# Block 2: log gates one panel earlier, first softmax ahead of a weight remainder, decays inside the attention, squares added before they are summed

## The reference, cut to what matters

```python
# block 1 (RWKV + dilated attention + FFN), then block 2, two layers of
h = h + 0.5 * rmsnorm(swiglu(rmsnorm(h, g_pre_ffn1), w_ffn1_gu, w_ffn1_down), g_post_ffn1)
h = h + rmsnorm(token_mixer(rmsnorm(h, g_pre_mix), ...), g_post_mix)
h = h + 0.5 * rmsnorm(swiglu(rmsnorm(h, g_pre_ffn2), w_ffn2_gu, w_ffn2_down), g_post_ffn2)
# token_mixer
fq, fk, fv, ff, gq, gk, gv, ga, gr, g_merge_a, g_merge_b = split(h @ w_in)
log_f = log_sigmoid(ff + b_f)                         # forget gates, 8 heads
o_fox = fox_attention(fq, fk, fv, cumsum(log_f))      # softmax attention, 3 blocks of queries
log_a = log_sigmoid(ga @ w_alpha_up + b_alpha) / 16   # decays of the gated linear attention
o_gla = gla_chunked(gq, gk, gv, log_a)                # uses exp of cumsum(log_a), per chunk
y = (sigmoid(g_merge_a) * (o_fox @ w_fox_o) + sigmoid(g_merge_b) * (o_gla @ w_gla_o)) @ w_out
```

## Time and profile before

| | before |
|---|---|
| median of 3 runs | 2022.82 us (2022.75, 2022.82, 2027.86) |
| the profiled execution | 2027.96 us, its span 2026.1 us |
| PE busy | 1910.9 us, 94% |
| DVE busy | 1402.3 us, 69% |
| ACT busy | 908.5 us, 45% |
| POOL busy | 102.4 us, 5% |

### The profile page before, as it was taken

How to read it: one execution, slowest core, us unless ns; L and a number is a source line. 1 busy time by engine, 2 the same in 40 slices (tenths; PEclk the granted TensorE clock), 3 DMA queues, 4 the chain that set the end, 5 groups by cost and what they waited for, 6 DMA issues and landing times.

```text
span 2026.1 us, 36336 instructions
## 1 busy us (share of the span) xinstructions
PE 1910.9 (94%) x14822; PEld 1860.5 (92%) x14822; DVE 1402.3 (69%) x2171; ACT 908.5 (45%) x1345; POOL 102.4 (5%) x164
## 2 busy tenths in 40 slices
PE   7897899998799999999899999999999989999997
PEld 7896788988799999999899999999999989999997
DVE  6997576677766567656767777756765676777764
ACT  3443444443555454444546444434443454544442
POOL 0201021200000000002100000000000200000000
PEclk7998888998899999999999999999999999999999
DMA  9684020003355535553323535543554333454552
GB/s 359 254 307 152 31 75 1 1 1 128 118 183 190 193 136 176 181 193 126 115 103 110 178 136 180 188 170 128 184 182 174 132 101 109 146 187 146 186 194 98
DMA packets 41435, 301.47 MB, mean 149 GB/s; under 512 B 4512, under 2 KB 6704, under 8 KB 7264
## 3 DMA queue, kind: packets, MB, share of 16 engines
q1 hardware_dynamic: 40720, 296.90, 41.6%
q0 software_dynamic: 592, 2.87, 0.4%
HBM read 298.70 MB, written 1.05 MB: 148 GB/s over the span
## 4 chain that ended last, share of the span: by engine, by line
PE 79%; DVE 12%; DVEq 4%; ACT 2%; issue 1%; DMA 1%; POOL 0%; SPq 0%; ACTq 0%; POOLq 0%
PE acc L718 20%; PE acc L720 19%; PE acc L719 19%; DVE w_lo L700 3%; ACT w_hi L693 1%; PE acc L744 1%; PE acc L745 1%; PE acc L748 1%; PE mb L733 1%; PE mb L720 1%; PE mb L718 1%; PE mb L719 1%; PE mb L2048 1%; PE acc L2048 1%; DVEq L858 1%
## 5 line engine op out<-in xcount | busy, mean ns | idle before, releaser
L718 PE MATMUL acc<-h_hi,w_hi 128*128 128x272 f32 (+1 forms) x2752 | 795.0, 289 | 22.0 <-DVE w_lo L700 12.1
L720 PE MATMUL acc<-h_hi,w_lo 128*128 128x272 f32 (+1 forms) x2752 | 788.1, 286 | 0.0
L719 PE MATMUL acc<-h_lo,w_hi 128*128 128x272 f32 (+1 forms) x2752 | 786.6, 286 | 0.0
L700 DVE TENSOR_TENSOR w_lo<-land,w_hi 128x2048 fp32r<-128x2048 f32 (+1 forms) x243 | 586.2, 2412 | 148.9 <-ACT w_hi L693 148.1
L693 ACT ACTIVATE w_hi<-land 128x2048 fp32r<-128x2048 f32 (+1 forms) x243 | 488.6, 2011 | 429.6 <-PE acc L720 376.9
L718 PEld LDWEIGHTS acc<-h_hi,w_hi 128*128 128x128 f32 x2752 | 522.7, 190 | 27.3 <-DVE w_lo L700 14.5
L719 PEld LDWEIGHTS acc<-h_lo,w_hi 128*128 128x128 f32 x2752 | 522.2, 190 | 0.4 <-issue 0.2
L720 PEld LDWEIGHTS acc<-h_hi,w_lo 128*128 128x128 f32 x2752 | 522.6, 190 | 0.0
L718 PE MATMUL acc<-a_hi,w_hi 128*128 128x272 f32 (+1 forms) x880 | 251.7, 286 | 0.7 <-DVE w_lo L700 0.5
L719 PE MATMUL acc<-a_lo,w_hi 128*128 128x272 f32 (+1 forms) x880 | 250.3, 284 | 0.0
L720 PE MATMUL acc<-a_hi,w_lo 128*128 128x272 f32 (+1 forms) x880 | 250.3, 284 | 0.0
(11 more groups left out here) (560 smaller groups left out, 2785.6 us busy)
## 6 DMA issues: line engine op xcount, KB each, us to landing
land<-in_w_gu SPq DMA_DIRECT2D x110, 1024.0 KB, 4.8
land<-in_w_in SPq DMA_DIRECT2D x67, 1024.0 KB, 4.8
land<-in_w_down SPq DMA_DIRECT2D x40, 1408.0 KB, 6.0
ada_first<-in_w_ada SPq DMA_DIRECT2D x24, 1024.0 KB, 8.4
land<-in_w_ab SPq DMA_DIRECT2D x12, 1024.0 KB, 4.9
land<-in_w_out SPq DMA_DIRECT2D x12, 1024.0 KB, 4.8
const<-in_const POOLq DMA_DIRECT2D x1, 1134.0 KB, 9.2
x<-in_x SPq DMA_DIRECT2D x1, 1024.0 KB, 5.7
```

Source lines behind the costliest of these rows:

```text
L700: k.nc.vector.tensor_tensor(weights_lo(k, p, c), k.land[:, p.par, c], weights_hi(k, p, c).bitcast(F32), ALU.subtract).then_inc(k.lo_ready, 1)
L718: mm(out, weights_hi(k, p, c), hi, start=start, stop=False)
L719: mm(out, weights_hi(k, p, c), lo, start=False, stop=False)
L720: return mm(out, weights_lo(k, p, c), hi, start=False, stop=stop)
```

## The change

Four edits, in block 2 alone:

- In stage z, PE sums three squares instead of nine. DVE first adds the tiles of `f` in pairs (three additions of two tiles each), signals `z_total`, and PE takes the two totals before its last tile t = 7.
- The gates: what ACT did for them at i = 3 and 4 it now does at 2 and 3, and DVE's part moves up likewise; `cum_ready` is signalled at i = 4, ahead of that step's remainder. The single panel goes to the second half of its accumulator bank, and PE starts the attention after panel 5 has been taken out (`count(1)`). Chunk 0 needs no more than that either.
- The remainder of mixed panel 1 moves from step i = 6 to behind the first softmax (`normalised(0)`).
- The running sums and decays of the linear attention move to the ends of the attention steps 1, 3 and 5 (`dve_gla_decay`), ACT's exponentials of them from step 2 to 6, and four of the eight `dve_undo` to step 7; the other four stand at i = 3.

```diff
 def pe_project_z(k, pe, b, start, count, W):
-    square_sum()
+    pe.wait_ge(k.sq_ready, z_squares(b) + 1)
+    mm(k.mb[:, 2, 0:n], k.mean_ones[:, :], k.sq[:, 0, W], start=True, stop=False)
     for t in range(KT):
+        if t == KT - 1:
+            pe.wait_ge(k.z_total, b)
+            mm(k.mb[:, 2, 0:n], k.mean_ones[:, :], k.f[:, 0, W], start=False, stop=False)
+            mm(k.mb[:, 2, 0:n], k.mean_ones[:, :], k.f[:, 1, W], start=False, stop=True).then_inc(k.z_sums, 1)
...
-        if t >= SUMS_BEHIND:
-            square_sum()
-    while done < KT:
-        square_sum()
-    square_sum().then_inc(k.z_sums, 1)
...
 def dve_z(k, dve, b, W, gain, start, size):
+    def squares(to, more):
+        dve.wait_ge(k.sq_ready, z_squares(b) + more + 3)
+        two = k.f[:, to:to + 2, W]
+        return v.tensor_tensor(two, two, k.f[:, more:more + 2, W], ALU.add)
+    squares(0, 2)
     for t in range(*Z_GROUPS[4]):
         rest(t)
+    squares(4, 6)
+    dve.drain()
+    squares(0, 4).then_inc(k.z_total, 1)
     split_lo(k, dve, Panel.of(start + 2), size)
...
 def pe_chunk(k, pe, l, c):
-    if o == 1 or r == 0:
+    if r == 0:
+        pe.wait_ge(k.acc_free, p.count(1 + o))
+    elif o == 1:
         pe.wait_ge(k.acc_free, p.count(2))
...
 def pe_mixer(k, pe, l):
-    pe.wait_ge(k.acc_free, mixed_panel(l, 0).count(2))
+    pe.wait_ge(k.acc_free, mixed_panel(l, 0).count(1))
     pe.wait_ge(k.cum_ready, l + 1)
...
 def act_mixer(k, act, l):
-        if q == 2:
+        if q == 6:
             act_gla_decay(k, act, l)
...
 def dve_mixer(k, dve, l):
     masked(0)
     normalised(0)
+    split_lo(k, dve, mixed_panel(l, 1), IN_K)
     for q in range(n_steps + 1):
...
         dve_chunk_split(k, dve, l, q)
+        if q in (1, 3, 5):
+            dve_gla_decay(k, dve, l, q // 2)
+        elif q == 7:
+            for t in range(4, KT):
+                dve_undo(k, W2, t)
```

More of the change, by code:

```diff
@@ L542, in semaphores @@
     k.z_sums = sem("z_sums")
+    k.z_total = sem("z_total")
     k.scale_root = sem("scale_root")
@@ L726, in pe_project_z @@
     mm = k.nc.tensor.matmul
[L727 to L735, removed]
     two = [Panel.of(start + i) for i in range(2)]
@@ L759, in pe_project_z, with pe_project @@
         pe_project(k, pe, start + 4, count - 4, 2, W)
-def pe_project(k, pe, start, count, tiles, W, ready=None):
+def pe_project(k, pe, start, count, tiles, W, ready=None, first=0):
     n = W.stop - W.start
@@ L771, in one @@
             for t in range(KT):
-                last = tile_mm(k, out_bank(k, p, o, n), p, o * KT + t, k.h_hi[:, t, W],
+                last = tile_mm(k, out_bank(k, p, o + first, n), p, o * KT + t, k.h_hi[:, t, W],
                                k.h_lo[:, t, W], t == 0, t == KT - 1)
@@ L1173, in dve_products_z @@
     section(dve, start, count, one, ("next", None), unrolled=True)
-SUMS_BEHIND = 2
 Z_GROUPS = ((0, 1), (1, 2), (2, 4), (4, 6), (6, 8))
@@ L2519, in pe_gates2 @@
     last.then_inc(k.dec_mm, 1)
+assert all(Panel.of(M_LAYER + l * L_PANELS + L_IN + IN2_EARLY - 1).bank == 1 for l in range(LAYERS))
 def early_sizes(i):
@@ L2533, in act_in_early @@
                      early_sizes(3 if i == 0 else i + 2))
-        if i == 3:
+        if i == 2:
             act.wait_ge(k.dec_mm, l + 1)
@@ L2539, in act_in_early @@
             act.drain().then_inc(k.dec_abs, 1)
-        elif i == 4:
+        elif i == 3:
             a(k.lf[0:8, :], k.lf[0:8, :], ACT.Exp, scale=-1.0)
@@ L2564, in dve_in_early @@
         dve.wait_ge(k.panel_done, p.count(3))
-        v.tensor_tensor(k.in2[:, 2 * i:2 * i + tiles, :], out_banks(k, p, TOK, tiles), over(k.scale[:, :], tiles),
+        v.tensor_tensor(k.in2[:, 2 * i:2 * i + tiles, :], out_banks(k, p, TOK)[:, 2 - tiles:2], over(k.scale[:, :], tiles),
                         ALU.mult).then_inc(k.acc_free, 1)
+        if i == 4:
+            dve.wait_ge(k.dec_exp, l + 1)
+            v.tensor_tensor(k.lf[0:8, :], k.cum[0:8, :], k.lf[0:8, :], ALU.subtract)
+            dve.drain()
+            v.tensor_tensor_scan(k.cum[0:8, :], k.e2[0:8, 0, :], k.lf[0:8, :], 0.0, ALU.mult, ALU.add)
+            dve.drain()
+            dve.wait_ge(k.fox_copy, l * FOX_PAIRS + 1)
+            v.tensor_copy(k.chl[CUM_HI, :], k.cum[0:8, :])
+            dve.drain()
+            v.tensor_tensor(k.chl[CUM_LO, :], k.cum[0:8, :], k.chl[CUM_HI, :].bitcast(F32),
+                            ALU.subtract).then_inc(k.cum_ready, 1)
+        if i == IN2_EARLY - 1:
+            break
         if i != 1:
@@ L2569, in dve_in_early @@
         if i == 2:
-            for half in range(2):
-                dve_undo_root(k, W2, half)
             dve.drain()
[L2573 to L2576, removed]
             v.tensor_scalar(k.cum[0:8, :], k.small[FF_ROWS, :], vec(k, "b_f", layer=l, rows=FF_ROWS), 0.0, ALU.add,
@@ L2582, in dve_in_early @@
             v.memset(k.e2[:, :, :], 1.0)
+            for half in range(2):
+                dve_undo_root(k, W2, half)
             dve.drain()
-        elif i == 5:
-            dve.wait_ge(k.dec_exp, l + 1)
-            v.tensor_tensor(k.lf[0:8, :], k.cum[0:8, :], k.lf[0:8, :], ALU.subtract)
-            v.tensor_tensor(k.e1[:, :, :], k.gcum[:, :, :], k.e1[:, :, :], ALU.subtract)
[L2588 to L2592, removed]
+        elif i == 3:
+            for t in range(4):
+                dve_undo(k, W2, t)
+            dve.drain()
+        elif i == 4:
+            v.tensor_tensor(k.e1[:, :, :], k.gcum[:, :, :], k.e1[:, :, :], ALU.subtract)
@@ L2593, in dve_in_early @@
             v.memset(k.e2[:, :, 0:TOK:GLA_C], 0.0)
             dve.drain()
[L2595 to L2612, removed]
@@ new lines, in dve_gla_decay @@
+def dve_gla_decay(k, dve, l, step):
+    v = k.nc.vector
+    if step == 0:
+        for t in range(2):
+            v.tensor_tensor_scan(k.gcum[:, t, :], k.e2[:, t, :], k.e1[:, t, :], 0.0, ALU.mult, ALU.add)
+        dve.drain()
+    else:
+        t = step - 1
+        g = k.gcum[:, t, :].rearrange("p (n c) -> p n c", n=GLA_N)
+        mid = g[:, :, GLA_C // 2:GLA_C // 2 + 1]
+        v.tensor_tensor(k.e2[:, t, :].rearrange("p (n c) -> p n c", n=GLA_N), g,
+                        mid.broadcast_to([P, GLA_N, GLA_C]), ALU.subtract)
+        v.tensor_copy(k.gst[:, t, 0, :], mid.rearrange("p n c -> p (n c)"))
+        v.tensor_copy(k.gst[:, t, 1, :], g[:, :, GLA_C - 1:GLA_C].rearrange("p n c -> p (n c)"))
+        v.tensor_tensor(k.gst[:, t, 2, :], g[:, :, GLA_C - 1:GLA_C].rearrange("p n c -> p (n c)"),
+                        mid.rearrange("p n c -> p (n c)"), ALU.subtract)
+        dve.drain()
+        last = v.tensor_scalar(k.e2[:, t, :], k.e2[:, t, :], 80.0 * 16, -80.0 * 16, ALU.min, ALU.max)
+        if step == 2:
+            last.then_inc(k.gz_ready, 1)
@@ L3151, in program_tensor @@
         for i in range(3, IN2_EARLY):
-            pe_project(k, pe, base + L_IN + i, 1, early_sizes(i) // KT, W2)
+            tiles = early_sizes(i) // KT
+            pe_project(k, pe, base + L_IN + i, 1, tiles, W2, first=2 - tiles)
         pe_mixer(k, pe, l)
```

## The result

The changed kernel takes **1995.42 us** (median of 4 runs, 1994.97 to 1997.12) against 2022.78 us beside it (4 runs, 2022.26 to 2027.86): a ratio of 0.9861, 95% interval 0.9844 to 0.9878, 27.4 us less. Forecast were 1992.4 and 30.4 less. The profiled execution took 1994.97 us, its span 1993.1.

The account below looks back on a forecast made before the run. PE was taken as the bound, four fifths of the chain that ended last. Stage z 16 us plus the attention's starts 6.75 and 7.7 gave 30.4 us off the median 2022.82: 1992.4 us, range 1986 to 1998 (chance 0.60).

Parts of the forecast that it names:

- Stage z, 16 us: Stage z: PE drops six of nine sums, 2.7 us per stage over six stages, if the new wait doesn't hold it.
- The attention's start, 6.75 and 7.7 us: From PE's end of panel 6 to first products with values: gains in first and second layer, less new waits.
- the second step's wait: Attention's second step, first layer only: the softmax is ready about 0.7 us after PE wants it.
- slow clock: Attention's start: half-rate clock behind PE's 5.19 us wait, put at 2.5 us in the first layer, 2.2 in the second.
- new waits: Attention's start: PE waits for chunk 0's remainder, 0.45 us (second layer 0.25), and the first softmax, 0.85 us (1.25).
- Work moved into the attention, nothing: Attention steps 1, 3, 5, 7: 4.6 us of DVE work per layer costs nothing; bound 9.2 us for both layers.
- Rival B: Attention turns on DVE: late outputs delay masks and PE, all of the 9.2 us lost, 2001.6 us; chance 0.13.
- The sum: Whole kernel: 16 + 6.75 + 7.7 = 30.4 us, taken from the median 2022.82, giving 1992.4 us.
- C: Before the attention: POOL's late keys hold DVE's `cum`, the single panel's remainder and the next load; slower; chance 0.03.
- E: Attention's start: ACT's table switch takes longer than its 1.28 us row, up to 6.9 us, 1999.3 us; chance 0.06.
- its 1995.2 us: Forecast time by the skill page's 1.38 us drain with each table switch: the sum would be 2.8 us smaller.

Follow-up runs that it names:

- experiments 8 and 9: Changed kernel with two more 128x544 DVE additions per stage z: 2001.40 us; changed kernel with PE summing two squares instead of three, DVE adding the totals: 1992.29 us.

## Why the prediction was right

**Stage z, 16 us.** Right in size and mechanism: 2.75 per clean stage (forecast 2.7), covers of 0.43 and 0.28 us (0.3 and 0.25), shown to be real by experiments 8 and 9.

**The attention's start, 6.75 and 7.7 us.** Measured 6.87 and 7.40 up to the first products with values; the second step's wait, 0.18 us instead of 0.7, lies behind them, so that the forecast for this stretch alone was 7.45 in the first layer. The mechanism is right: no wait for panel 6, no slow clock, and small new waits in its place. That the sum agrees so well is in part luck.

- Both new waits came out as forecast since both of their sides were late. In the first layer PE wanted chunk 0 at 1.06 us after panel 6 and its remainder ended at 1.48 (forecast 0.85 and 1.30), so the wait was 0.47 (0.45). PE was through chunk 0 at 4.82 and the softmax was there at 5.62 (4.33 and 4.98): a wait of 0.80, with the second head 1.00 (0.85). In the second layer they were 0.38 and 0.93 (0.25 and 1.25).
- The slow clock was put too high. Without its waits the start now takes 9.93 - 1.47 = 8.46 and 10.92 - 1.31 = 9.61 us, where I had 8.05 and 9.1. So the half clock had cost some 2.1 and 1.7 us, not 2.5 and 2.2. The smaller waits at the second step and in the second layer make up for it.
- ACT was late for a reason that I didn't have. I had `w_hi` end 2.0 us after panel 6, held by PE as before. It ended 2.8 us after (979.60 against 976.83), held by its load: the single panel's remainder frees the buffer at 971.04 + 1.32, and the load lands 5.3 us later.

DVE in the changed kernel, first layer: `cum`, the single panel's remainder, chunk 0's remainder.

```profile
970.15 0.29 DVE L2579 CAST chl<-cum 8x272 fp32r<-8x272 f32 x1 [0.25 <-POOL fkz L2670]
...
971.04 1.32 DVE L701 TENSOR_TENSOR w_lo<-land,w_hi 128x1024 fp32r<-128x1024 f32 x1
...
976.02 2.29 DVE L701 TENSOR_TENSOR w_lo<-land,w_hi 128x2048 fp32r<-128x2048 f32 x1 [1.28 <-ACT w_hi L694]
```

What each edit is worth also differs from what one would think: that the mask is free of the decays is worth 8.3 us, the moved remainder 3.4, the early start at panel 6 nothing. They overlap, since in each the next limit, ACT, takes over. The earlier gates were not taken out by themselves.

**Work moved into the attention, nothing.** Right: at most 0.3 us of a bound of 9.2. Rival B is out.

**The sum.** The rows give 6 x 2.73 + 6.87 + 7.40 - 0.3 = 30.4 us, the forecast's number (the second step's 0.18 is in the 0.3); that it agrees to the tenth is luck. The whole second block bears it out: from the first stage z to the end it took 1298.0 us before and 1263.8 after, and of these 34.2 us the three more starred stages before are worth 4 to 5, which leaves about 30. The medians give 27.4 and, on another chip, 27.9. About 1 us of the difference may be the wait for the last store, 1.9 us in the profile before and 2.9 in the one after; in the other twelve it is 1.9 four times and 3.0 to 3.4 eight times, and why it changes I haven't tested. The rest I can't place: on a single chip the kernel before took from 2015.95 to 2029.10 us, at mean granted clocks of 0.971 and 0.961. To go from the median and not from the profile was needed: the two profiles differ by 33.0 us of span, in good part since the one before has four starred stages and the one after has one.

**Rivals C and E.** `cum` waited 0.25 us for POOL's keys and the single panel's remainder ended 1.4 us before PE wanted it, so PE never stood there; what C named behind it, the next load, is what now holds ACT, for 0.6 to 1.0 us of PE's time in the two profiles of the changed kernel. E is out: ACT's last copy ends at 979.86 + 0.25 = 980.11, the table's load ends at 980.12 + 1.28 = 981.40, and the exponential starts at 981.42. The Trainium skill ("ScalarE: Activation LUTs", What ACT_TABLE_LOAD costs) adds 1.38 us for a drain to each switch to another set; these rows show none. That its 1995.2 us lies near the measured median is chance.

## What to carry to other kernels

Ask of each removed wait what is late next, and of the whole set of edits which one the next limit hides: here an early start was worth nothing until a 1.28 us table load was moved, and a microsecond per layer afterwards. Adding on an idle engine to save products on a busy one pays until its cover is used up; two covers of 0.43 and 0.28 us, read from the rows, told where. Where executions differ by more than an edit is worth, compare the same stage in several traces.

## What the runs showed of the hardware

The same stage with the same wait in front of it (1.13 us at the first square of the fourth stage z) began at a granted clock of 1.00 in some executions and had a mean of 0.66 over five microseconds in others, some 1.4 us longer. The Trainium skill ("TensorE: Matmul & The Clock Gate", Part 1: The HAM clock gate) says of a kernel's start that the number of products at half rate differs from run to run; the traces agree for stages deep in the program: the changed kernel had one such stage of six in one execution and three in another. With eight thrown-away products in the gap, 1.0 us of PE, none of twelve did. That PE's standing brings the fall about is thus shown for this place only as far as none of 12 against 25 of 72 can. In the attention's start the clock fell behind all four waits of 5.19 us and behind 2.15, 3.10 and 3.60 us, and not behind 0.80, 0.93, 1.26, 1.72, 1.89 and, in the run with the squares alone, 2.09.
